# Prompt attention: value products ahead of the sliding-window scores in each step

## What is computed

```python
s_c = einsum('bqghd,bngd->bghqn', q, kc) * scale + bias    # 63 compressed keys
o_c = softmax(s_c, masked) @ vc
s_s = einsum('bqghd,bgqkld->bghqkl', q, k_sel) * scale + bias  # 16 selected blocks of 64
o_s = softmax(s_s, masked) @ v_sel
s_w = einsum('bqghd,bkgd->bghqk', q, kw) * scale + bias    # window of 512
o_w = softmax(s_w, masked) @ vw
o = g[..., 0:1] * o_c + g[..., 1:2] * o_s + g[..., 2:3] * o_w
```

## Time and profile before

| | |
|---|---|
| median of three runs (lowest, highest) | 2273.68 us (2272.06, 2279.49) |
| the profiled execution, its own time | 2271.01 us |
| its span, first to last instruction | 2269.2 us |
| mean granted clock of TensorE over the span | 0.953 of full speed; 1.00 in each round of the stage after the first |
| TensorE busy over the span | 2082.9 us (92%) |
| stage of prompt attention | 578 to 870 us |
| a round of pair (0,7), (1,6), (2,5), (3,4) | 16.73, 17.92, 18.65, 18.94 us |

### The profile page before, as it was taken

One profiled execution on the slowest core, in us unless ns is written; L12 is line 12 of the kernel. 1 busy time (PEld: TensorE's weight loads), 2 busy tenths in 40 slices (PEclk: granted clock), 3 DMA queues, 4 the chain that ended last, 5 costly groups with the idle time before them and its releaser, 6 DMA issues. The chain is left out here.

```text
span 2269.2 us, 33313 instructions
## 1 busy us (share of the span) xinstructions
PE 2082.9 (92%) x13581; PEld 1937.6 (85%) x13581; DVE 746.0 (33%) x1439; ACT 503.9 (22%) x917; POOL 571.6 (25%) x471
## 2 busy tenths in 40 slices
PE   6999999985688887999999799999999999997897
PEld 5999989953566776888879799999999999997786
DVE  3202533333766764111132343202321321234412
ACT  4112011122466564101021231110000000011323
POOL 1222400000344443112213213333323333331120
PEclk6999999987799998999999799999999999998898
DMA  5323264124200001111113121111111111113011
GB/s 165 113 75 125 53 217 161 62 110 166 82 1 2 2 1 29 48 44 42 42 46 111 49 94 46 37 56 47 44 42 54 47 35 58 47 35 126 24 46 77
DMA packets 164786, 150.88 MB, mean 66 GB/s; under 512 B 24747, under 2 KB 157389, under 8 KB 161934
## 3 DMA queue, kind: packets, MB, share of 16 engines
q1 hardware_dynamic: 160846, 111.68, 16.2%
q0 software_dynamic: 2304, 33.56, 3.7%
q10 hardware_dynamic: 1536, 4.23, 0.5%
HBM read 132.54 MB, written 21.10 MB: 68 GB/s over the span
## 5 line engine op out<-in xcount | busy, mean ns | idle before, releaser
L583 POOL CAST WS<-W 128x1024 fp32r<-128x1024 f32 (+2 forms) x126 | 124.7, 990 | 1139.8 <-PE ffn_acc L575 539.9
L575 PE MATMUL ffn_acc<-HH,WS 128*128 128x344 f32 x2112 | 394.8, 321 | 9.0 <-DVE HL L507 7.9
L575 PEld LDWEIGHTS ffn_acc<-HH,WS 128*128 128x128 f32 x2112 | 344.3, 189 | 9.4 <-issue 8.0
L585 POOL TENSOR_TENSOR WS<-W,WS 128x1024 fp32r<-128x1024 f32 (+2 forms) x126 | 297.2, 2358 | 10.1
L575 PE MATMUL ffn_acc<-HL,WS 128*128 128x344 f32 x1056 | 224.8, 321 | 0.0
L575 PE MATMUL ffn_acc<-AH,WS 128*128 128x344 f32 x1056 | 195.4, 320 | 0.0
L575 PE MATMUL proj_acc<-HH,WS 128*128 128x344 f32 x912 | 174.2, 323 | 6.2 <-DVE HL L507 6.2
L575 PEld LDWEIGHTS ffn_acc<-HL,WS 128*128 128x128 f32 x1056 | 179.4, 190 | 0.0
L575 PEld LDWEIGHTS ffn_acc<-AH,WS 128*128 128x128 f32 x1056 | 171.6, 188 | 0.0
L1844 POOL TENSOR_SCALAR Hr<-Hr,tiny,gtok 128x63 f32<-128x63 f32 (+4 forms) x192 | 124.4, 657 | 174.5 <-DVE tiny L1924 141.7
L575 PE MATMUL merge_acc<-HH,WS 128*128 128x344 f32 x768 | 149.6, 327 | 11.8 <-POOL WS L585 11.8
(11 more groups left out here) (374 smaller groups left out, 3163.6 us busy)
## 6 DMA issues: line engine op xcount, KB each, us to landing
W<-in_w_in SPq DMA_DIRECT2D x31, 512.0 KB, 4.1
W<-in_w_ffn_gate SPq DMA_DIRECT2D x22, 512.0 KB, 3.8
W<-in_w_ffn_up SPq DMA_DIRECT2D x22, 512.0 KB, 3.9
X<-kept_x SPq DMA_DIRECT2D x2, 4128.0 KB, 13.3
W<-in_w_ffn_down SPq DMA_DIRECT2D x16, 384.0 KB, 3.4
W<-in_w_ffn_down SPq DMA_DIRECT2D x16, 320.0 KB, 3.1
kept_x<-Z SPq DMA_DIRECT2D x1, 4128.0 KB, 15.6
Z<-kept_x SPq DMA_DIRECT2D x1, 4128.0 KB, 13.8
```

Of the source, the lines that this page charges most:

```text
L575: last = k.nc.tensor.matmul(acc[:, s, n, 0:NW], k.WS[:, ws, part, c, :], src[:, c, n * NW:(n + 1) * NW], start=(c == 0 and part == 0 and s ...
L583: k.nc.gpsimd.tensor_copy(k.WS[:, ws, 0, 0:nk, :], w).then_inc(hi_done, 1)
L585: k.nc.gpsimd.tensor_tensor(k.WS[:, ws, 1, 0:nk, :], w, k.WS[:, ws, 0, 0:nk, :].bitcast(F32), ALU.subtract).then_inc(split_done, 1)
```

## The change

In the list of TensorE the value products of a step stand between the selected and the window scores; before, they stood behind both. Nothing else differs, on no engine.

```diff
             for s in range(S):
                 selected_scores(s)
-                window_scores(s)
                 if s % 2 == 0 and s >= 4:
                     products(s // 2 - 2, 1)
                 if s % 2 == 1 and s >= 3:
                     products(s // 2 - 1, 0)
+                window_scores(s)
                 if s:
                     turns(s - 1)
```

## The result

The change makes the kernel slower: 2284.18 us, the median of 20 runs (2277.16 to 2297.92), against 2270.13 us of 20 runs before. The ratio is 1.0061, its 95% interval 1.0048 to 1.0074; that is 13.8 us. The forecast was 2267.5, a gain of 6.2 us, and at most 2276.

A forecast was written before the change was run, and what follows sets the result against it. TensorE was taken to stand at window scores awaiting ScalarE (25.3 us) and transposes awaiting GpSimd (18.9). Terms by tile pair, 1.8 - 3.2 - 2.4 - 2.4 = -6.2 us, took the median 2273.7 to 2267.5; range 2257 to 2276.

The forecast's parts named there:

- First step: nothing: First of a round's four steps: no gain, its end hangs on VectorE's chain; at most 0.1 us lost in tile pair (3,4).
- first steps as long as before: Sign that the forecast is right: the first step of each four-step round keeps its length.
- a gain would need a shorter VectorE chain: Lower bound for a round's first step: no part of the change shortens VectorE's copy, queries, minima and reciprocal, so no gain.
- the loop L: From third step's window scores through VectorE's minima and ScalarE's exponentials to the fourth's window scores: 3.9 us.
- Second step: Second of a round's four steps: products wait for ScalarE's group 1 copy, losing 0.45 us in pair 3, 0.48 in pair 4.
- Third and fourth step: Last two of a round's four steps, together: +0.6, -0.8, -1.0, -1.2 us per round in tile pairs (0,7), (1,6), (2,5), (3,4).
- Clean removal: Rival, chance 0.15: waits of third and fourth steps vanish and none takes their place; 16 us gained, 2257.5 us.
- Slower: Rival, chance 0.10: the window loop decides in every tile pair, through VectorE's queue; 12.7 us lost, 2286 us.
- Nothing: Rival, chance 0.10: what the window wait wins comes back wholly at the transposes' wait for GpSimd; 2273.7 us.

The follow-up runs named there:

- the filled standstill: Changed kernel with 14 idle identity transposes put where TensorE waits for GpSimd in first steps; run twice: 2275.39 and 2273.51 us, ratios 1.0017 and 1.0009.
- all_but_first: Kernel before the change, with products ahead of window scores in second, third and fourth steps only; 2270.58 us, ratio 1.0007.
- after: The changed kernel, products ahead of window scores in all steps, against the kernel ahead of the change; 2284.18 us, ratio 1.0061.
- first_only: Kernel before the change, with products ahead of window scores in first steps only; 2282.37 against 2268.98 us, ratio 1.0057.
- late_34: Kernel before the change, with products ahead of window scores in third and fourth steps only; 2269.17 against 2270.47 us, ratio 0.999.
- before: The kernel ahead of the change, products behind the window scores in every step; 2270.13 us, median of 20 runs.

## Why the prediction was wrong

The step that failed is the first term of the sum, "First step: nothing". The terms of the other steps held, but for small sizes.

- *First step: nothing.* Wrong twice; its sign "first steps as long as before" failed too. First, "What the window scores waited here comes back whole as a longer wait for GpSimd" was right as a wait (18.9 to 36.0 us) and taken to be free. But after one standstill of mostly 1.9 to 2.7 us, in place of two of at most 1.5, the clock fell in eight rounds: 12.6 us, more than the 11.4 by which the stage grew from its second round on. That the clock is the cause is shown by the order in first steps alone (seven falls, nearly the whole loss, rounds without a fall as long as before) and by the filled standstill (no fall, 10 to 12 us back). Second, "a gain would need a shorter VectorE chain", and from above 0.1: the chain got longer, by 0.37, 0.65, 0.36 and 0.57 us in pairs 1 to 4, some 7 us in 14 rounds. GpSimd's selected factor hangs on a reciprocal (L1918) that VectorE's queue holds behind the window minima; those came later in the fourth step, as the loop L said, and the factor fell on the scaling. Third and fourth steps alone show it without a fall of the clock.
- *Second step.* +0.42 us in pair 3, and +0.44 in pair 4 by all_but_first, since in after no such step of its whole rounds is free of a fall; forecast +0.45 and +0.48. Nothing in pair 1 and +0.13 in pair 2. The new wait of the products for ScalarE's copy is there: in all_but_first 0.37 us in pair 3 and 0.46 to 0.95 in pair 4, in seven rounds and not in eight, since the first round of pair 3 still works on a tile of four groups. It goes when the copy goes first.
- *Third and fourth step.* Forecast +0.6, -0.8, -1.0, -1.2; measured +0.39, -0.87, -1.01, -1.23. The loop is the limit as worked out, in pair 1 too, at 3.84 us for 3.9.
- *The rivals.* Clean removal (0.46, 1.33, 1.24 and 1.03 us off the two steps) came in pair 4 alone; elsewhere the loop stood in the way, as the prediction said. "Slower" had the right sign and a price near the measured time (2286), but by luck: its mechanism was window loops that decide in every pair, and third and fourth steps got shorter in three of four. Its remark that the factor for GpSimd comes later behind the minima was true. No rival had the clock. "Nothing" came near the rest: without the falls the stage would be about 1.2 us shorter.

What stays open is what decides between a fall and none. The same standstill in the same pair is followed by a fall in one round and by none in another: in first_only a fall followed 1.5 us, in late_34 none followed 1.75. In all_but_first two rounds with two standstills fell too. Shown is, in one profile of each kernel and two of the filled one, that the rounds of before with their two short standstills kept the clock, that joining the two loses it in many rounds, and that work put into the standstill keeps it. How many falls the other executions had is not on record.

## What to carry to other kernels

A wait that is only moved is not free when it joins another one: two short standstills of TensorE with work between them can be cheaper than one of their sum, because the granted clock may fall after the long one; look at the clock by steps, not at its mean over the span (0.953 and 0.947 here). When a chain on the slower side is declared untouched, check which instructions of other engines now run beside it, since a GpSimd instruction can stretch one of VectorE's without a wait in the trace (0.29 to 1.02 us). And take the chain's own work away first: the reordering lost 14 us alone and was worth 18 with the query work moved out of the first step.

## What the runs showed that was not expected

A VectorE scaling of 64x256 that takes 0.29 us took up to 1.02 us beside a GpSimd scaling of 128x896 and ended 0.14 us after it, while in the form with an accumulator it took 0.41 us with no such spread. TensorE's granted clock went to 1.2 GHz after standstills of 1.5 to 2.7 us in rounds that are otherwise busy, and some 200 idle transposes more made the stage of after, from its second round on, 12 us shorter.
